# Moving one key subtraction and the head sums one group later in VectorE's attention program

## The reference

```
proj = h @ w_in                       # q | k | v | z | f, 16 heads of 64
c = cumsum(log_sigmoid(f + b_f))      # per head, over tokens
logits = q.k / 8 + c[t] - c[s]        # causal mask
o = softmax(logits) @ v               # per head
y = (o * silu(z)) @ w_out
```

## Time and profile before

| | us |
|---|---|
| median of 3 runs | 678.89 (678.32 to 680.39) |
| the profiled execution, time | 680.2 |
| the profiled execution, span | 678.4 |
| PE busy | 638.2 (94%) |
| DVE busy | 414.5 (61%) |
| ACT busy | 334.8 (49%) |
| POOL busy | 313.3 (46%) |

### The profile page before, as it was taken

One profiled execution on the slowest core, in us unless ns is written; L12 is line 12 of the kernel. 1 busy time (PEld: TensorE's weight loads), 2 busy tenths in 40 slices (PEclk: granted clock), 3 DMA queues, 4 the chain that ended last, 5 costly groups with the idle time before them and its releaser, 6 DMA issues.

```text
span 678.4 us, 9386 instructions
## 1 busy us (share of the span) xinstructions
PE 638.2 (94%) x2960; PEld 517.7 (76%) x2960; DVE 414.5 (61%) x801; ACT 334.8 (49%) x569; POOL 313.3 (46%) x412
## 2 busy tenths in 40 slices
PE   4979899999999999899988999999999999999897
PEld 1767787787878787688766778888888888887676
DVE  6657786867878687646686863424333343366864
ACT  7646575655655575455546553223231331455451
POOL 6465455656365455100176737564536643001771
PEclk9999999999999999899999999999999999999999
DMA  6234343333333343135001313332223232250032
GB/s 225 92 100 115 122 127 118 102 100 124 116 107 114 117 123 104 32 112 170 30 32 62 102 53 125 124 98 88 90 95 124 82 128 101 86 170 25 31 113 74
DMA packets 27161, 68.69 MB, mean 101 GB/s; under 512 B 3568, under 2 KB 10096, under 8 KB 27136
## 3 DMA queue, kind: packets, MB, share of 16 engines
q1 hardware_dynamic: 27136, 68.37, 30.9%
HBM read 66.23 MB, written 2.13 MB: 101 GB/s over the span
## 4 chain that ended last, share of the span: by engine, by line
PE 63%; DVE 16%; issue 9%; ACT 6%; POOL 3%; DMA 1%; DVEq 0%; SPq 0%; ACTq 0%; POOLq 0%
PE ps_pj L1062 18%; PE ps_pj L1064 18%; PE ps_pj L1063 18%; POOL w_lo L412 3%; DVE act_lo L954 2%; PE ps_tr L1071 2%; DVE k_st L871 2%; DVE xT L950 1%; ACT logit L523 1%; ACT k_st L569 1%; DVE logit L807 1%; DVE o_u L819 1%; DVE t_a L997 1%; PE ps_tr L1062 1%; DVE q_lo L863 1%
## 5 line engine op out<-in xcount | busy, mean ns | idle before, releaser
L412 POOL TENSOR_TENSOR w_lo<-w_raw,w_hi 128x256 fp32r<-128x256 f32 x324 | 256.1, 824 | 142.8 <-ACT w_hi L470 142.7
L1062 PE MATMUL ps_pj<-act_hi,w_hi 128*128 128x512 f32 (+1 forms) x744 | 297.5, 400 | 10.8 <-DVE act_lo L954 4.4
L1064 PE MATMUL ps_pj<-act_hi,w_lo 128*128 128x512 f32 (+1 forms) x744 | 290.1, 390 | 0.0
L1063 PE MATMUL ps_pj<-act_lo,w_hi 128*128 128x512 f32 (+1 forms) x744 | 289.4, 389 | 0.0
L1062 PEld LDWEIGHTS ps_pj<-act_hi,w_hi 128*128 128x128 f32 x744 | 140.7, 189 | 44.0 <-issue 9.6
L1064 PEld LDWEIGHTS ps_pj<-act_hi,w_lo 128*128 128x128 f32 x744 | 140.2, 189 | 29.7
L1063 PEld LDWEIGHTS ps_pj<-act_lo,w_hi 128*128 128x128 f32 x744 | 140.8, 189 | 24.7
L470 ACT CAST w_hi<-w_raw 128x1024 fp32r<-128x1024 f32 x96 | 100.0, 1049 | 80.3 <-DMA w_raw<-in_weights 67.5
L445 POOL TENSOR_TENSOR acc<-acc,sq 128x512 f32<-128x512 f32 x14 | 21.3, 1524 | 123.0 <-ACT sq L615 122.1
L420 POOL TENSOR_TENSOR bias<-bias,future 128x128 f32<-128x128 f32 x64 | 34.3, 568 | 80.5 <-DMA bias<-negc_scratch 80.5
L523 ACT ACTIVATE logit<-logit,nmax 128x128 f32<-128x128 f32 (+1 forms) x64 | 36.2, 565 | 60.1 <-DVE nmax L798 59.9
(11 more groups left out here) (141 smaller groups left out, 778.4 us busy)
## 6 DMA issues: line engine op xcount, KB each, us to landing
w_raw<-in_weights SPq DMA_DIRECT2D x100, 512.0 KB, 3.4
bias<-negc_scratch SPq DMA_DIRECT2D x16, 256.0 KB, 7.3
bias<-negc_scratch SPq DMA_DIRECT2D x16, 192.0 KB, 6.2
xT<-in_xT SPq DMA_DIRECT2D x8, 256.0 KB, 5.9
bias<-negc_scratch SPq DMA_DIRECT2D x16, 128.0 KB, 4.8
out<-xT SPq DMA_DIRECT2D x7, 256.0 KB, 2.0
bias<-negc_scratch SPq DMA_DIRECT2D x16, 64.0 KB, 3.4
p_in<-in_pT SPq DMA_DIRECT2D x2, 512.0 KB, 4.5
```

The lines of the kernel that those rows point to most:

```text
L412: last = nc.gpsimd.tensor_tensor(w_lo[place % RING][:, tiles], w_raw[stream(place) % RAW][:, tiles], w_hi[place % RING][:, tiles], ALU.sub ...
L1062: nc.tensor.matmul(out, w_h, a[0][:, k, tokens], start=k == first, stop=False)
L1063: nc.tensor.matmul(out, w_h, a[1][:, k, tokens], start=False, stop=False)
L1064: end = nc.tensor.matmul(out, w_l, a[0][:, k, tokens], start=False, stop=k == last)
```

## The change

Of the two key subtractions, head 0's stays in group 9 and head 1's stands in group 10, behind normalise(7) and pt_rest(5); each has the wait for `k_hi_done` ahead of it. `head_sum(0)` stands in group 10 and `head_sum(1)` in group 15, by `g - 1 in SUM_AT`. Nothing else is changed: `SUM_AT` itself is not, by which ScalarE's `head_half` goes. (The few words that name the change say "in group 9 instead of 10"; in the diff it is head 1's subtraction that goes from 9 to 10.)

```diff
-                    if g == 9 and project:
+                    if g in (9, 10) and project:
+                        h = g - 9
                         dve.wait_ge(k_hi_done, m + 1)
-                        for h in range(2):
-                            own, other = slice(h * DH, h * DH + DH), slice(DH - h * DH, 2 * DH - h * DH)
-                            last = nc.vector.tensor_tensor(k_st[b][h][other, :], scaled[1][own, :],
-                                                           k_st[b][h][own, :], ALU.subtract)
-                        last.then_inc(qk_ready, 1)
-                    if attend and g in SUM_AT:
-                        head_sum(SUM_AT[g], m0, jj)
+                        own, other = slice(h * DH, h * DH + DH), slice(DH - h * DH, 2 * DH - h * DH)
+                        last = nc.vector.tensor_tensor(k_st[b][h][other, :], scaled[1][own, :],
+                                                       k_st[b][h][own, :], ALU.subtract)
+                        if h == 1:
+                            last.then_inc(qk_ready, 1)
+                    if attend and g - 1 in SUM_AT:
+                        head_sum(SUM_AT[g - 1], m0, jj)
```

## The result

The changed kernel takes 674.86 us (median of 7 runs, 672.48 to 677.26) against 678.89 us (677.61 to 680.39): ratio 0.994, 95% interval 0.9923 to 0.9957. It is faster, by 4.0 us, half of the 8.0 us that the walk gave; the forecast was 671.2, and the measured time lies 0.14 us inside the upper end of the range (668.4 to 675.0). The profiled execution took 674.86 us with a span of 673.1, 5.3 less than the span of before.

The account below looks back on a forecast made before the run. TensorE bounds the kernel, losing at most 10.3 us ahead of unit 7's transposes to VectorE's L807. Gains of 0.9 + 0.9 + 0.9 + 4.4 + 0.9 = 8.0 us gave 670.9 from the median, forecast as 671.2; range 668.4 to 675.0.

Parts of the forecast that it names:

- the walk: VectorE's instructions followed turn by turn from k0 to pt_rest(7) under the new order: 8.0 us gained in all.
- the signs that the prediction set for itself: Transposes' wait gone in turns 2, 4 to 7; value product's 0.3 us only in turns 1 to 3; period down 0.8 or more.
- Turn 1: Transposes gain 1.32 us, wait for ScalarE's hi part 0.26, new value-product stall 0.35: 0.9 us gained.
- the 0.9: Turn 8: transposes start 1.1 us earlier, pt_rest(7) can't follow fully, value product at 286.24 instead of 287.14: 0.9 us gained.
- the terms for turns 2 to 4: Gains of 0.9 us each in turns 2 and 3, and 1.1 us in turn 4.
- the same walk with their own starts: Turns 2 and 3, walked like turn 1: transposes gain 1.3 and 1.15 us, value product held 0.35 and 0.3.
- rival A: Stall moves to the value product or ScalarE's chain in every turn: 4.9 us gained, 674.0 us; chance 0.26.
- The terms for turns 4 to 7: The whole 1.10 us wait ahead of unit 7's transposes goes each turn: 1.1 a turn, 4.4 us for four.
- rival E: TensorE's lower clock in turn 8, some 1.7 us, left unchanged; were it gone, 669.5 us; chance 0.08 together with B.

Follow-up runs that it names:

- the new order of GpSimd: GpSimd's mask(m, 0) moved behind the third weight slot of its turn, against the kernels after and before: 669.02 and 671.88 us.
- before_again: The kernel before, unchanged, run once more for a second trace: 677.06 us.
- after_again: The changed kernel, unchanged, run once more for a second trace: 671.76 us.
- light_before: Kernel before, GpSimd leaving out three of four weight instructions per slot (first three slots apart): 667.49 us, ratio 0.9824.
- light_after: Changed kernel, GpSimd leaving out three of four weight instructions per slot (first three slots apart): 665.62 us, ratio 0.9812.
- k_g13_scale: Changed kernel with VectorE's scale(2) and both key subtractions moved behind pt_rest(7): 679.35 us, ratio 1.0016 to before.

## Why the prediction was half right

The time came into the range, but by 0.14 us and with half of the gain, and by the signs that the prediction set for itself the forecast failed: the periods of the laps to turns 2 to 4 fell by less than 0.8 us, the wait ahead of the transposes was to be gone in turns 2 and 4 and was 0.50 and 0.20, and a wait of the value product took the place of the rest, which it did in turns 4, 6 and 7 too (0.32, 0.15 and 0.25), where it was to be absent.

**What was right.** The place (VectorE's L807 ahead of unit 7's transposes), that the two moves free it, the durations of VectorE's stretch (the product took 0.49 where 0.6 was assumed), and that the value product would be held by pt_rest(7) next. Turn 1 was walked rightly: 0.26 us idle ahead of the value product shown, 0.35 forecast, and the distance between its two value products fell from 12.41 to 11.66 us, 0.75 where I took 0.9. In time it brought next to nothing: turn 1's first value product came 0.67 us later than before (63.22 against 62.55), with waits for L798 of 2.09 and 1.22 us ahead of turn 1's scores where before shows one of 1.81. In turn 8 VectorE now does this (as the earlier trace rows):

```profile
278.75 0.16 DVE L805 RECIPROCAL rrec<-rsum 128x1 f32<-128x1 f32 x1 [0.68 <-ACT logit L523]
278.95 0.49 DVE L807 TENSOR_SCALAR logit<-logit,rrec 128x512 f32<-128x512 f32 x1
...
280.10 0.67 DVE L819 TENSOR_TENSOR o_u<-ps_o,o_half 64x512 f32<-64x512 f32 x1
```

Its two value products came to stand 7.10 us apart instead of 7.62; in the second traces 7.12 and 7.95. That is 0.5 to 0.8 for the 0.9.

**Where it failed.** In the terms for turns 2 to 4: 0.9 + 0.9 + 1.1 forecast, 0.09 + 0.18 + 0.23 in this pair of traces. The step is "the same walk with their own starts". I let k0 start where it started before, against TensorE, and walked only from there on. But VectorE's start is itself the end of its lap, and GpSimd, held by its bias DMAs, does not keep its place in it. The masks ahead of turn 2's value product start at 105.05 in after, 0.87 us ahead of it, and at 102.89 in before, 3.20 ahead; in turn 6 it is 3.51 and 7.84. So GpSimd's two weight slots fell on VectorE's group 15, and the slot behind the next masks on the query subtractions. I had named this mechanism in rival A ("their place against VectorE shifts by up to 1.1 us a turn"), with 674.0 us and a chance of 0.26. Its sum is near what came, 674.86, but not its pattern: A leaves about 0.6 us of gain in every turn, and the traces have next to none up to turn 4 and nearly the full gain from 5 on. I priced it only between k0 and pt_rest(7), where it cost nothing (the product even got rid of its meeting), and not in the 24 us ahead of k0, where all of the 1.43 us were. The light kernels and the laps under the new order of GpSimd show the cause; that bias DMAs set GpSimd's place is read from its waits, and why its masks came 2.2 us later in turn 2 of after than of before is open.

**The terms for turns 4 to 7.** Those of the laps to turns 5 to 7 were 1.1 each and measured 1.06, 0.94 and 0.77. A part of this is luck of the base: with `before_again` against `after_again` the same laps differ by 0.44, 0.63 and 0.71, and those to turns 2 to 4 by 0.69, 0.07 and 0.07. From the one trace of before I took a wait of 1.10 us as fixed.

**The clock, rival E.** The profiled execution of before has the granted clock at 0.89 from 264 to 280 us; after and both second traces have 1.00 there:

```profile
264.00:280.00 16.00, 13.75 (x62) 10.82 (x62) 11.84 (x43) 7.24 (x20) 5.18 (x8) 0.89 0.30 99
```

```profile
264.00:280.00 16.00, 13.60 (x74) 10.93 (x74) 11.44 (x46) 8.13 (x23) 5.21 (x8) 1.00 0.33 93
```

(first before, then `before_again`; columns as in the earlier trace rows). Before, turn 8's first value product came 18.32 us behind turn 7's second one, in `before_again` 16.73, in after 16.94. So about 1.4 us of the 5.3 us between the two spans go with this stretch; it comes and goes with the same program. That 5.3 - 1.4 is near the 4.0 us of the medians proves nothing, for the traces differ in more. Before has a second stretch at the half clock in turn 1 (granted clock 0.50 from 49.35 to 52.75, behind TensorE's wait of 1.81 us), and `before_again` has one there too, a little later (0.89 over 60 to 76). After has none from 30 to 290 us, though it waited 2.09 us in the same place. `light_before` has the stretch of turn 8 too (17.77), `light_after` not (16.29); with one trace each nothing follows for the order.

**Left open.** What decides in an execution whether GpSimd falls beside the wrong instructions (the start of the bias DMAs, their landing), and so why after spreads over 4.8 us in 7 runs. Which of the losses of `k_g13_scale` counts most. What ends TensorE's full clock in turn 8 of one execution and not of another.

## What to carry to other kernels

When a wait is taken from the bound engine, walk the whole lap of the engine that it waited for, not only the stretch that was edited: an engine that is tied to DMAs need not move along with the rest, and what it meets is new. Two engines that lengthen each other's instructions are best looked at by grouping one engine's instructions in a good and in a bad lap; here three groups held all of 1.43 us. Before reordering the engine that is late, see what lengthens it: one line of GpSimd's order was worth more than the reordering of VectorE, in part because it also took away a plain wait. And a wait read from one execution is one draw: between the same two value products, two traces of one kernel differed by 4.4 us, 1.6 of them in the stretch where one ran for a while at the half clock.

## What the hardware showed that I had not expected

The engines do not meet only at semaphores, as the opening of this document has it. GpSimd's subtractions in SBUF cost VectorE more than a slowed product. Query subtractions of 64x512 took 0.96 us in the mean in one lap and 0.72 in another, L880 took 1.30 and 1.05, with a floor of 0.69; instructions with an operand in PSUM (L798, L830, L813) agreed within 0.01 us. The Trainium skill ("SBUF — State Buffer", section "SBUF: two separate sides") states the lock for VectorE instructions with two SBUF inputs against GpSimd ones that read SBUF; the three groups that grew between the two laps are of this kind. Two more of this kind did not grow (L857 and L871, 0.69 in both laps); in the longer lap no GpSimd instruction ran beside them. The same section of the Trainium skill names a second kind, instructions in a 2-port mode. The product L807, which reads one tile and a column, grew too: for 128x256 it took 0.35 us at 115.09 with GpSimd idle, and 0.93 at 127.94 beside two weight instructions, in both laps alike; whether it runs in that mode no run here shows. GpSimd pays too: four masks took 1.70 us at 105.05 in after and 2.62 beside the key subtractions of `k_g13_scale`. The whole price in this attention is the difference of before and `light_before`, 11.3 us by their medians, though that one holds whatever else GpSimd's weights cost outside the attention: the six laps to turns 2 to 7 alone give 186.24 - 178.32 = 7.9 us, and with `before_again` 183.07 - 178.32 = 4.8 us.
